# A 32,000-instruction transformer kernel: attention rebuilt around row tiles, transferred rotations and transposed value products

## The reference, cut to what matters

```python
q = qkv[..., :QK_WIDTH].reshape(B, S, N_HEADS, 2, HEAD_DIM)      # 8 heads, 2 components of 64
k = qkv[..., QK_WIDTH:2 * QK_WIDTH].reshape(B, S, N_HEADS, 2, HEAD_DIM)
v = qkv[..., 2 * QK_WIDTH:].reshape(B, S, N_HEADS, V_DIM)        # V_DIM = 128
q = apply_partial_rope(q, cos, sin) * (HEAD_DIM ** -0.5)         # first 16 of 64 features rotate
k = apply_partial_rope(k, cos, sin)
s = einsum('bqhcd,bkhcd->bhcqk', q, k)                           # masked: key <= query
p = softmax(s)
a = p[:, :, 0] - lam * p[:, :, 1]
o = einsum('bhqk,bkhe->bqhe', a, v)
o = rmsnorm(o, subln_g) * (1.0 - lambda_init)                    # over the 128 features of a head
return o.reshape(B, S, V_WIDTH) @ w_o
```

## Time and profile before

| | |
|---|---|
| median of 3 runs | 2737.68 us (2737.57 to 2739.07) |
| the profiled execution's own time | 2739.36 us |
| its span, first to last instruction | 2737.6 us |
| PE busy | 2622.0 us, 96% of the span, 13220 matmuls |
| DVE, ACT, POOL busy | 50%, 40%, 43% |
| mean granted TensorE clock | 0.974 of full speed |

### The profile page before, as it was taken

The page is one execution under the profiler, slowest core; times in us unless marked ns, Lnnn a source line. Parts: engine busy times, 40 slices in busy tenths (PEclk is TensorE's granted clock), DMA queues, the critical chain, the costliest instruction groups (busy, mean ns, idle before and its releaser), DMA issues.

```text
span 2737.6 us, 32521 instructions
## 1 busy us (share of the span) xinstructions
PE 2622.0 (96%) x13220; PEld 2211.1 (81%) x13220; DVE 1381.2 (50%) x2103; ACT 1102.5 (40%) x1897; POOL 1175.3 (43%) x634
## 2 busy tenths in 40 slices
PE   7998999999999999998999998899999899899997
PEld 5887888888888888886887786888888787888886
DVE  6775360433344604337564573662553575661654
ACT  5554451333324423324553453542443453542432
POOL 3232474344445744442334232544446323544443
PEclk9998999999999999998999998999999899999998
DMA  4121243332332333322222221223323112223322
GB/s 142 51 62 31 72 113 98 95 100 78 93 100 80 105 93 100 93 66 75 69 69 72 70 70 51 73 84 109 95 88 95 29 46 76 72 86 108 100 87 68
DMA packets 434983, 223.29 MB, mean 82 GB/s; under 512 B 14353, under 2 KB 433297, under 8 KB 434833
## 3 DMA queue, kind: packets, MB, share of 16 engines
q1 hardware_dynamic: 434832, 221.20, 28.3%
HBM read 219.07 MB, written 2.10 MB: 81 GB/s over the span
## 4 chain that ended last, share of the span: by engine, by line
PE 91%; DVE 5%; ACT 1%; POOL 1%; issue 1%; DMA 0%; SPq 0%; DVEq 0%; POOLq 0%; ACTq 0%
PE ps L519 29%; PE ps L520 28%; PE ps L521 28%; PE ps L2471 1%; PE ps L2457 1%; PE ps L1473 1%; PE ps L2478 1%; DVE cb L700 0%; PE ps L1526 0%; PE ps L1398 0%; DMA xT<-in_xT 0%; PE ps L2459 0%; DVE acc L1456 0%; PE ps L2496 0%; DVE tmp L2705 0%
## 5 line engine op out<-in xcount | busy, mean ns | idle before, releaser
L493 POOL TENSOR_TENSOR wl<-stg,wh 128x1024 fp32r<-128x1024 f32 (+4 forms) x447 | 1003.3, 2251 | 1284.1 <-ACT wh L485 1278.3
L519 PE MATMUL ps<-hh,wh 128*128 128x512 f32 (+1 forms) x2308 | 869.6, 377 | 35.2 <-DVE hl L1047 11.0
L521 PE MATMUL ps<-hh,wl 128*128 128x512 f32 (+1 forms) x2308 | 856.7, 371 | 0.0
L520 PE MATMUL ps<-hl,wh 128*128 128x512 f32 (+1 forms) x2308 | 855.9, 371 | 0.0
L485 ACT ACTIVATE wh<-stg 128x1024 fp32r<-128x1024 f32 (+4 forms) x447 | 435.1, 984 | 310.0 <-DMA stg<-in_mlp_w_down 109.7
L519 PEld LDWEIGHTS ps<-hh,wh 128*128 128x128 f32 x2308 | 436.5, 189 | 115.3 <-issue 21.5
L519 PE MATMUL ps<-bh,wh 128*128 128x512 f32 (+1 forms) x1304 | 490.3, 376 | 18.5 <-DVE acc L762 10.7
L521 PEld LDWEIGHTS ps<-hh,wl 128*128 128x128 f32 x2308 | 436.2, 189 | 75.4
L520 PEld LDWEIGHTS ps<-hl,wh 128*128 128x128 f32 x2308 | 436.8, 189 | 74.1 <-issue 2.9
L520 PE MATMUL ps<-bl,wh 128*128 128x512 f32 (+1 forms) x1304 | 486.5, 373 | 0.0
L521 PE MATMUL ps<-bh,wl 128*128 128x512 f32 (+1 forms) x1304 | 486.3, 373 | 0.0
(11 more groups left out here) (302 smaller groups left out, 2844.1 us busy)
## 6 DMA issues: line engine op xcount, KB each, us to landing
stg<-in_ffn_up SPq DMA_DIRECT2D x88, 512.0 KB, 3.8
stg<-in_mlp_w_up SPq DMA_DIRECT2D x64, 512.0 KB, 4.1
stg<-in_mlp_w_down SPq DMA_DIRECT2D x64, 512.0 KB, 4.0
stg<-in_ssd_in_proj SPq DMA_DIRECT2D x48, 512.0 KB, 3.9
stg<-in_attn_w_qkv SPq DMA_DIRECT2D x24, 512.0 KB, 3.9
stg<-in_conv_w_in SPq DMA_DIRECT2D x24, 512.0 KB, 3.7
stg<-in_ffn_down SPq DMA_DIRECT2D x32, 384.0 KB, 3.4
stg<-in_ffn_down SPq DMA_DIRECT2D x32, 320.0 KB, 3.2
```

What stands on the lines that cost most here:

```text
L493: pool.tensor_tensor(wl[:, slab.slot, w], stg[:, slab.slot, w], wh[:, slab.slot, w].bitcast(F32), ALU.subtract).then_inc(s.lo_done, 1)
L519: pe.matmul(po, lh, rh, start=start, stop=False)
L520: pe.matmul(po, lh, rl, start=False, stop=False)
L521: return pe.matmul(po, ll, rh, start=False, stop=stop)
```

## The change

It has four parts, and it changes no other section.

1. **Scores from row tiles.** Q is stored once. The products of component 0 use rows 0 to 63 of the array, those of component 1 rows 64 to 127, issued in turn and into different banks. For heads 1 to 6 the block (component 1, queries 1) moves from bank 4 to bank 6, for which PE waits for the head's exponentials before the K projection.
2. **Rotation by transfers.** `rot`, `turn` and the zero fills go. SP issues four transfers of 8 rows by 512 columns within SBUF for each of Q and K, behind a slab load in its list; DVE's first rope product now reads SBUF twice.
3. **Values as weights.** V is the stationary operand and the attention weights move: 4 key blocks of 512, 384, 256 and 128 columns, 12 products. The output has features on the partitions, so `out_transposed` goes. The sums of squares need four one-column PE products (`out_sums`), and the reciprocal root is spread back by four PE transposes (`out_spread`). Two of eight output tiles of the attention (`begin(2, ...)`) are computed in steps inside the last head.
4. **Banks and the ssd's end.** `bank_free` waits only for the last user of its bank. In the ssd section slabs are split earlier, two more output tiles are begun in the gaps of the last group (`part`), the second output stage uses six slots, and DVE's order in `shifted_vector` changes.

```diff
     def scores(self, pe, h):
-        pe.wait_ge(s.qk_lo, 3 * h + 3)
-        if h == 0:
-            pe.wait_ge(s.q_zero, 4)
-        for b in ORDER:
...
+        pe.wait_ge(s.qk_lo, 2 * h + 2)
+        for b in (3, 2):
+            self.score_products(pe, h, b)
+        self.score_masks(pe, h, ((0, 3), (1, 3), (0, 2), (1, 2)))
+        self.score_products(pe, h, 0)
+        if h > 0:
+            pe.wait_ge(s.o_kept, h)
+        if 0 < h < HEADS - 1:
+            self.score_products(pe, h, 1)
+            self.score_masks(pe, h, ((0, 0), (1, 0), (0, 1), (1, 1)))
...
+    def score_products(self, pe, h, b, components=(0, 1)):
+        for q, k in ((bh, bh), (bh, bl), (bl, bh)):
+            for c in components:
+                bank, off = score_place(h, c, b)
+                rows = slice(64 * c, 64 * c + 64)
+                pe.matmul(ps[:, bank, off:off + (b + 1) * P], q[rows, self.Q_, b * P:(b + 1) * P],
+                          k[rows, self.K_, 0:(b + 1) * P], start=q is bh and k is bh, stop=False,
...
     def values(self, pe, h):
...
+        for kt in range(TB):
+            t, off = TRI[kt]
+            w, k = slice(off, off + (TB - kt) * P), slice(kt * P, (kt + 1) * P)
+            end = product(pe, ps[:, 4, kt * P:T], bh[:, self.V_, k], bl[:, self.V_, k],
+                          bh[:, self.A_ + t, w], bl[:, self.A_ + t, w], kt == 0, kt == TB - 1)
-    def turn(self, pe, h):
...
+    def rotate(self, sp, h, c):
+        sp.wait_ge(s.raw_done, 3 * h + c + 1)
+        if h:
+            sp.wait_ge(s.rope_done, 6 * h + 3 * c - 3)
+        else:
+            sp.wait_ge(s.lam_sum, 4)
+        for base in (0, 64):
+            for half in range(2):
+                to, src = (slice(base + x * HALF_ROT, base + (x + 1) * HALF_ROT) for x in (half, 1 - half))
+                sp.dma_start(tmp[to, 3 + c, :], tmp[src, c, :]).then_inc(s.rotated[c], 16)
...
+    def out_sums(self, pe, h, v_head):
+        pe.wait_ge(s.v_lo, TB * v_head + TB)
+        pe.wait_ge(s.o_sq, h + 1)
+        for b in range(TB):
+            end = pe.matmul(ps[:, 7, b:b + 1], self.squares[:, b * P:(b + 1) * P], ones[:, 0:1], start=b == 0,
...
+    def out_spread(self, pe, h):
+        pe.wait_ge(s.o_rstd, h + 1)
+        for b in range(TB):
+            end = pe.transpose(ps[:, 7, b * P:(b + 1) * P], orstd[:, b:b + 1].to_broadcast([P, P]), ident)
...
         def body(h, before):                       # PE
             self.scores(pe, h)
             if before:
-                self.out_transposed(pe, h - 1, h)
+                self.out_sums(pe, h - 1, h)
                 self.project(pe, h + 1, 0)
+                self.out_spread(pe, h - 1)
+                pe.wait_ge(s.exp_done, 8 * h + 8)
             self.project(pe, h + 1, 1)
             self.probs_turned(pe, h)
-            self.turn(pe, h + 1)
             if before:
-                pe.wait_ge(s.ot_lo, h + SEED)
+                pe.wait_ge(s.o_norm, h)
...
+        out = self.out.together(pe)
         self.scores(pe, HEADS - 1)
-        self.out_transposed(pe, HEADS - 2, HEADS - 1)
+        self.out_sums(pe, HEADS - 2, HEADS - 1)
+        for n in range(HEADS - 2):
+            next(out)
+            if n == 2:
+                self.out_spread(pe, HEADS - 2)
         self.probs_turned(pe, HEADS - 1)
+        next(out)
         self.values(pe, HEADS - 1)
...
         def body(h, before):                       # DVE
             self.softmax(dve, h)
+            self.rope(dve, h + 1, 0)
+            if before:
+                self.out_scaled(dve, h - 1)
+            self.probs_lo(dve, h)
+            self.rope(dve, h + 1, 1)
+            self.qk_lo(dve, h + 1)
             if before:
                 self.out_lo(dve, h - 1)
...
     def bank_free(self, pe, half, n):              # Crossing
         d = self.dense
-        if half == 1 or d.parts == 1:
-            pe.wait_ge(s.acc_done, SEED + d.before + d.full)
-        else:
-            pe.wait_ge(s.acc_done, SEED + d.before + n - 3)
+        users = [m + 1 for m in range(d.full) if d.bank_of(m) == self.bank[half, n]]
+        pe.wait_ge(s.acc_done, SEED + d.before + max(users, default=1))
...
             else:                                  # Ssd.tensor, second half
+                pe.wait_ge(s.e_done, 16 * (self.g0 + 3) + 16)
+                self.out.part(pe, 3, 6)
                 self.group_sums(pe, 3, 1)
-            self.group_spread(pe, 3)
+                self.out.part(pe, 4, 3)
+                self.group_spread(pe, 3)
+                self.out.part(pe, 4, 6)
...
+                        if k < 2 and not ahead:    # Ssd.scalar
+                            split.hi(act, self.out.st.first + TABLES - 1 + k)
...
+                        if (self.i0, i, k) == (0, 3, 3):
+                            split.hi(act, self.out.st.first + self.out.early)
...
-                        if k == 1 and not ahead:
-                            split.hi(act, self.out.st.first + self.out.st.ring)
...
+                    if (self.i0, i) == (0, 3):     # Ssd.gpsimd, ahead of the group's power
+                        split.lo(pool, self.out.st.first + self.out.early)
...
+        def shifted_vector_early(self, dve):
+            for n in (4, 5):
+                self.shift_tile(dve, n)
+            self.shifted_out(dve, 4)
+            for n in (0, 1):
+                self.shift_tile(dve, n)
+            self.shifted_out(dve, 5)
+            for n in (6, 7):
+                self.shift_tile(dve, n)
+            for n in self.square_order():
+                self.shifted_sum(dve, n)
...
-            d = add(Dense(st_o, bh, bl, 1, att.ready, "copy", "squares", tail=2))
+            d = att.out = add(Dense(st_o, bh, bl, 1, att.ready, "copy", "squares", tail=2))
+            d.begin(2, (5, 6, 0, 1, 2, 3))
...
-                d.begin(3, ((3, 4, 5, 6, 3, 4, 5, 6), (0, 1, 2, 3, 0, 1))[half])
+                d.begin(3, ((3, 4, 5, 6, 3, 4, 5, 6), (0, 1, 2, 3, 4, 5))[half])
...
+            def behind(sp, n):                     # SP, behind slab n
+                h, c = divmod(n - RING - att.st.first, 3)
+                if 0 <= h < HEADS and c < 2:
+                    att.rotate(sp, h, c)
```

More of the change, by code:

```diff
@@ L87, in constant_columns @@
     at, n = {}, 0
-    for name, k in (("ident", P), ("ones", P), ("rot", P), ("rot2", P), ("mask", P), ("sel", SSD_H),
+    for name, k in (("ident", P), ("ones", P), ("rot2", P), ("mask", P), ("sel", SSD_H),
                     ("cos", T), ("sin", T)):
@@ L527, in multiply @@
         pe.wait_ge(s.lo_done, st.at(pos, i) + 1)
-        for j in range(k):
+        for j in range(j0, k):
             if ready:
```

212 lines of the change are left out of this document (107 added, 105 removed).

## The result

The changed kernel takes 2701.15 us (median of 4 runs, 2699.02 to 2702.72), 0.9863 of the kernel before (95% interval 0.9846 to 0.988), whose median beside it was 2738.4. It is faster by 37 us; 63 were forecast, and 2701 lies outside the range, 2662 to 2698. The profiled execution took 2702.44 us, its span is 2700.6, and its gain on the span of before (2737.6) is 37.0. Run a second time, unedited, it had a median of 2694.9 and a ratio of 0.9842 (0.9825 to 0.9858); the median of all eight runs, 2693.65 to 2702.72, is 2699.4. One kernel's times thus scatter by 9 us.

What follows compares the result with a forecast made beforehand. PE was taken as the bound, busy throughout heads 1 to 6; gains of 22.8, 2.8, 11, 6, 14.6, 4 and 1.6 sum to 62.8 us, giving 2675 us, range 2662 to 2698.

Steps and rivals of the forecast that it cites:

- DVE's additions met POOL's at the ssd crossing: Rival: DVE's shifts and sums collide with POOL's additions, cutting the ssd gains; 2684 us, chance 0.15.
- Heads 1 to 6: Attention heads: 3.8 us saved per head, a head of 24.3 us if PE never waits; 22.8 us for six.
- Does PE wait then? Three places.: Heads 1 to 6: checked `probs_turned`, the K projection and K's rotation for PE waits; expected none.
- Scores become 3.0: Each head's scores: overlapping row halves plus switches cut 4.73 us to 3.0, bounds 2.6 and 4.7; gain 1.7.
- The rotation rival: Rotated rows land 8 us after K's projection, PE waits 2.6 us in seven heads; 2693 to 2700 us, chance 0.15.
- I take 4.5: Heads: K's rotated rows land 4.5 us after its projection, under the 5.4 allowed, hidden with 0.9 us to spare.
- Head 7: Last head and output tiles: six of eight tile steps move into PE's idle time; gain 11 us, bounds 8 and 13.
- The chain behind it ... 26 to 28 us after scores: Last head: values, sums, root, spread, scaling and splitting done 26 to 28 us after scores, then one step.
- ssd, second half: Moved POOL splits, 6 us, and two tiles begun early, 8.6 us; together 14.6 us, bounds 8 to 19.
- So its 8.2 count and its 6.0 don't: ssd, second half: 8.2 us of early products count; the removed 6.0 us eviction wait doesn't, since DVE's work remains.
- Head 0: First head: shorter scores bring nothing as it waits for DVE; `turn` and values do, 2.8 us.
- Crossings: mla output's eviction wait goes and DVE follows at once, 4 us (1 to 5); two plain crossings give 1.6 us.

Runs made afterwards that it cites:

- scaled_first: Changed kernel with DVE scaling the previous head's output ahead of the rope of Q instead of behind it; 2696.84 us.
- full_rows: Changed kernel with each score product on all 128 rows instead of a half, output differs, for timing only; one run, 2704.92 us.
- step_behind_values: Changed kernel, last head: `probs_turned` after four output-tile steps instead of six, two behind it, the seventh behind values; 2690.77 us.
- before_banks: Kernel before the change with one edit, tail products wait only for the eviction that last used their bank; 2735.58 us, ratio 0.9985.

## Why the prediction was wrong

- **The direction and the main mechanisms** were right: PE's removed work counted where PE doesn't wait, and DVE's chain is the end at the ssd crossing. The sizes were not: 37 instead of 63 us. No rival took place as described, but each of two showed a part of itself: rotated rows landed late in some heads, and DVE's additions met POOL's at the ssd crossing.
- **Heads 1 to 6: 14.2 for 22.8.** The first step that failed is "Does PE wait then? Three places." There is a fourth. `out_scaled` moved behind the rope of Q on DVE, and PE's V projection waits for it. I had looked at K's rotation and taken Q's, which comes 5.9 us earlier and sooner meets DVE, as harmless. It leaves PE idle for 0.34 us a head, and costs 0.6 from start to start, as scaled_first shows (1.01 us from `probs_turned` to the V projection for 1.60); the two long heads are 2.3 longer, 2.0 of it this wait. The second step is "Scores become 3.0": 3.40, with 0.18 more ahead of them (V transposes 0.56 for 0.38). The products held, 2.3 us where half of 4.30 was 2.15; what was mis-sized are the masks, 0.43 by their columns and 0.79 by full_rows, where four in a row start 0.10 apart, and the changes of form, 0.48 for 0.4, of which 0.17 lies ahead of the scores. `turn` held: 142.12 to 150.42 before, 8.30 us, became 1.01 + 5.55 = 6.56 in scaled_first, 1.74 where I took 1.77; in the changed kernel it is 7.17, the difference being the wait. Values (1.43 for 1.4) and sums (0.86 for 1.0) held. Together that is 2.76 a head for 3.8.
- **The rotation rival** named a late landing of K. "I take 4.5", from the end of the projection, was near: 0.8 to the first issue and 4.0 to the landing, 4.8 for K in the undisturbed heads, under the bound of 5.4. The bound isn't always kept: in scaled_first one K took 6.0, and PE waited 1.15 us. The bound for Q wasn't worked out; DVE's combination ends at 133.01 in head 3, so it is 4.06 after the first issue, and anything later stops DVE.
- **Head 7: 7.1 for 11.8.** "The chain behind it ... 26 to 28 us after scores" was 30.8, since I let six steps "lie in the idle time" without counting them against it: PE's own work between scores and `probs_turned` became 15.7 us where the gap ended at 13.4. Nor did I name what stands behind the seventh step. step_behind_values shows that 24.8 was to be had.
- **ssd, second half: 9.8 for 14.6.** "So its 8.2 count and its 6.0 don't": the tiles count 5.9 for 8.6, and the rest 4 for 6. I had warned of the wait ahead of the sums and put it at 4 to 7 us; it is 11.8. ssd's first half (5.2 for 6) held.
- **Head 0: 2.8 for 2.8** has luck in it. The reasoning holds in the profile: from scores to `probs_turned` it takes 16.23 us for 16.27, and all of the gain lies behind. But in the twelve profiles with row halves and transfers, whose heads 0 are the same program but for the order of score products or transfers in some, it took 23.9 to 27.4 us, with 26.96 in the first. In the eight at 25.0 or less half clock begins near 40 us, with head 0's scores, and lies where PE would have waited for DVE; in the other four it falls behind that wait, where it counts.
- **Crossings: 5.6 forecast.** before_banks gives 3.2 between the medians, the ssd output included. That "DVE follows at once with its tail work" at mla missed that the sums wait for the same chain (4.70 us of wait became 4.13): 1.6 us for 4, and 0.3 where half clock fell longer behind it.
- **Half clock** was in the forecast only as a gain. The sum over the span fell from 63.2 to 56.3 us in one profile of the changed kernel and to 49.5 in the other, and the conv stretch, which the change hardly touches, lost 2.1 us by it. A range for a sum of such stretches should have had some 4 us to either side for this alone. And its upper end, 2698, lay below the 2700 that the rotation rival itself could give.

## What to carry to other kernels

Before counting a shortened stretch, write down for every wait that PE has left in it what stands ahead of the releasing instruction on its own engine; a removed PE instruction is worth its length only as far as the nearest of these allows. Work put into an idle gap has to be counted against the gap's length, and work with a late input goes behind the step that others wait for. Where waits bring half clock, compare stretches between fixed points in several profiles, and never one total.

## What was not expected of the hardware

- The clock fell to 1.2 GHz in heads where PE was busy throughout (window 98 to 100 above: busy 2.00 of 2.00, clock 0.50), 4.6 to 5.0 us after row-tiled scores began, at about 1.6 us of cost.
- The same wait of 1.57 us brought 1.7, 3.4 or 5.1 us of half-clock cost, with the same kernel too.
- Two row halves of the array ran as separate lanes: products three instructions apart started together (172.99, x2). Going into and out of this form cost 0.48 us a head, in four changes.
- Masks of 128 columns started 0.10 us apart when four stood in a row (full_rows, 0.40 us for four), about twice what columns alone take.
- Four transfers of 16 KB within SBUF take 2.65 us to issue and land 1.35 us after the last issue, behind a slab or ahead of it. Of 196 such groups in heads 1 to 7 of fourteen profiles, 166 landed within 4.1 us and 30 after 4.15 to 5.9. Every late one had an instruction transfer in its time or up to 0.8 us before, but 30 that landed in time had one too. The rows of Q that land in head 3 were late in 12 of the 14 profiles, so it is a place in the program and not chance. That the fetch is the cause is argued from this, and not shown.
- An addition of DVE between SBUF tiles took 2.72 us for 0.69 next to POOL's split.
